# Half sums joined by GpSimd in the short convolution of a two-layer encoder trunk

## Chip, cores and metric

One core of a Trainium2 chip (trn2). The metric is the device time of one launch in microseconds (us). All data are float32; the matmuls run on float32r operands.

## What is computed

The reference is a trunk of two layers on 256 tokens of width 2048. Each half of a layer is a modulated RMS norm, a mixer or MLP, and a gated residual sum. The change touches layer 0's mixer only:

```python
def short_conv_mixer(h, w_in, w_conv, w_out):
    b_gate, c_gate, v = jnp.split(h @ w_in, 3, axis=-1)
    u = dwconv_centred(c_gate * v, w_conv)
    return (b_gate * u) @ w_out

# in the trunk, for every layer and both of its halves
shift, scale, gate = modulation(i, s)        # silu(c) @ ada_w[i, s] + ada_b[i, s]
h = rms_norm(x, norm_g[i, s]) * (1.0 + scale) + shift
x = x + gate * out
```

## The kernel before

Activations lie feature by token: 16 blocks of 128 features by 256 tokens. The work is a list of units. One unit is one output block of 128 features: 2048 inputs, so 16 weight blocks of 128x128, in two halves of eight blocks. One half of a unit's weights (128x1024, 512 KB) is one DMA into one of four slots of `raw`.

Precision is kept by splitting. For each half h, ScalarE writes `wh` = raw rounded to float32r (`hi`, line 740), and VectorE writes `wl` = raw - wh (`lo`, line 1495). Activations are split likewise into two planes of `hcat` or `hid`, an upper and a lower one. A product is then upper x wh + lower x wh + upper x wl. TensorE has two forms for it:

- `single` (`block`, lines 1241 to 1243): three matmuls of 256 columns for each weight block, all into the same 256 columns of PSUM. The product is complete there, and the consumer reads it straight out of PSUM.
- `unit` (lines 1175 and 1178): one matmul of 512 columns (wh against both planes side by side) and one of 256 (wl against the upper plane). PSUM then holds two half sums, in columns 0 to 255 and 256 to 511, which must be added behind it.

The convolution has 48 units, three for each feature block: c, v and b. The first 15 are the head, done together. The other 33 (11 feature blocks, function `conv`, first feature block peeled, then a loop) use `single`, as do 14 of the 16 units of the output projection (`conv_out`); its first two run as a pair in two banks of their own. Units alternate between two PSUM banks, `psm[0]` and `psm[1]`. Slots: `hi(h)` waits until TensorE is done with half h-4, `lo(h)` waits for `hi(h)`, TensorE for `lo(h)`, and the DMA into the slot for `lo(h-4)`. The order on every engine is written by hand: every engine walks the same list of stages, each with its own function for it, and semaphores tie them.

During these stages VectorE has a second job: one tile of the modulation matrix for each unit (`tile`, line 1508, 128x2048, 1024 KB by DMA into two slots), whose one-column result GpSimd saves (`keep`, line 579). For a feature block VectorE also computes pad = c*v (line 1639), two shifted taps into acc (lines 1560 and 1563), and acc*b (line 1648). ScalarE copies c out of PSUM (line 859), makes the middle tap (line 791) and the rounded result (line 796); GpSimd makes the lower plane of the result (`lower`, line 590). In `conv_out` VectorE adds gate*product to x (line 1668), ScalarE squares x (line 778), GpSimd sums the squares (`add_square`, line 585), and `keep` follows.

## Time and profile before

| what | value |
|---|---|
| median of 3 runs | 2591.91 us (2591.65 to 2592.6) |
| profiled execution, own time | 2591.94 us |
| profiled execution, span | 2590.2 us |
| TensorE busy | 2533.1 us, 98% of the span |
| VectorE busy | 2090.9 us, 81% |
| ScalarE busy | 1377.7 us, 53% |
| GpSimd busy | 623.5 us, 24% |
| mean rate from HBM | 262 GB/s |
| chain that ended last | PE 87%, DVE 7%, DMA 2%, ACT 2% |

PE is TensorE, PEld its weight load, DVE VectorE, ACT ScalarE, POOL GpSimd, SP the DMA queue's engine. A row's duration is from its start to its end; the distance between starts of neighbouring rows of one engine is a little less, since they overlap at their ends. The own time is 1.74 us above the span, and 0.03 us above the median.

### The profile page before, as it was taken

Reading aid. Unit: us, or ns where it says so; the run is one execution under the profiler, and the core shown is the slowest. Engines: PE = TensorE matmul, PEld = TensorE weight load, DVE = VectorE, ACT = ScalarE, POOL = GpSimd, SP = SyncE. Lnnn points to the kernel's source line nnn. Section 1 sums busy time; section 2 is a strip of 40 time slices with the busy share of each in tenths; the row PEclk is TensorE's granted clock in tenths of the full one; section 3 lists DMA queues with packets and bytes.
Section 4 is the critical chain, followed back from the end, with each engine's and each line's share of the span. In section 5 each row is a group of like instructions: output and inputs, shape, how many; then the busy total and the mean of one; then the engine's idle time right before and its main releaser. Section 6 shows DMA issues by size and latency. Waiting matters only on the chain.

```text
span 2590.2 us, 45227 instructions
## 1 busy us (share of the span) xinstructions
PE 2533.1 (98%) x15518; PEld 2247.1 (87%) x15518; DVE 2090.9 (81%) x2637; ACT 1377.7 (53%) x2149; POOL 623.5 (24%) x576
## 2 busy tenths in 40 slices
PE   7899999999999999999999999999999999999998
PEld 6789999888888888888888888888888888888887
DVE  7988998998989989758899899998899655555554
ACT  4444444544544445556677746776754444444454
POOL 0011132333343343320011141113333111121123
PEclk8999999999999999999999999999999999999999
DMA  9979997798888888746656697664588655555554
GB/s 395 417 294 365 364 379 297 274 359 313 333 332 325 328 330 327 269 152 210 207 197 202 195 360 282 203 199 151 171 292 318 202 187 187 188 185 191 189 185 139
DMA packets 163917, 679.71 MB, mean 262 GB/s; under 512 B 18720, under 2 KB 18976, under 8 KB 139072
## 3 DMA queue, kind: packets, MB, share of 16 engines
q1 hardware_dynamic: 163728, 677.75, 73.0%
q8 instruction: 83, 1.36, 0.2%
q14 instruction: 58, 0.48, 0.1%
q0 software_dynamic: 48, 0.13, 0.0%
HBM read 675.58 MB, written 2.23 MB: 262 GB/s over the span
## 4 chain that ended last, share of the span: by engine, by line
PE 87%; DVE 7%; DMA 2%; ACT 2%; issue 1%; DVEq 0%; SPq 0%; POOL 0%; ACTq 0%; POOLq 0%
PE psm L1175 47%; PE psm L1178 23%; PE psm L1241 4%; PE psm L1243 3%; PE psm L1242 3%; DVE wl L1495 2%; DMA xs<-in_ada 1%; PE psr L1215 1%; PE psm L1460 1%; DVE adat L1508 1%; ACT wh L740 1%; DVE xs L1508 1%; PE psr L1377 1%; DMA raw<-in_w 1%; PE psr L1460 0%
## 5 line engine op out<-in xcount | busy, mean ns | idle before, releaser
L1495 DVE TENSOR_TENSOR wl<-raw,wh 128x1024 fp32r<-128x1024 f32 x854 | 1073.0, 1258 | 256.1 <-ACT wh L740 250.3
L740 ACT ACTIVATE wh<-raw 128x1024 fp32r<-128x1024 f32 x854 | 900.5, 1056 | 406.5 <-PE psm L1178 181.5
L1175 PE MATMUL psm<-hcat,wh 128*128 128x512 f32 x3120 | 986.2, 397 | 0.0
L1178 PEld LDWEIGHTS psm<-hcat,wl 128*128 128x128 f32 x3120 | 586.1, 188 | 138.5
L1175 PE MATMUL psm<-hid,wh 128*128 128x512 f32 x2240 | 703.6, 395 | 0.2 <-DVE wl L1495 0.2
L1178 PE MATMUL psm<-hcat,wl 128*128 128x256 f32 x3120 | 613.3, 278 | 0.0
L1178 PEld LDWEIGHTS psm<-hid,wl 128*128 128x128 f32 x2240 | 420.8, 188 | 99.5
L1175 PEld LDWEIGHTS psm<-hcat,wh 128*128 128x128 f32 x3120 | 476.1, 189 | 6.1 <-issue 5.3
L1508 DVE CUSTOM_DVE_ANT_0 adat<-adat,cond 128x2048 f32<-128x2048 f32 x176 | 463.0, 2631 | 16.4 <-DMA adat<-in_ada 16.3
L1178 PE MATMUL psm<-hid,wl 128*128 128x256 f32 x2240 | 440.0, 278 | 0.0
L1175 PEld LDWEIGHTS psm<-hid,wh 128*128 128x128 f32 x2240 | 340.9, 189 | 0.4 <-DVE wl L1495 0.4
L631 POOL TENSOR_TENSOR x<-x,tt 128x256 f32 (+1 forms) x140 | 183.0, 1307 | 343.3 <-DVE tt L1692 343.3
L579 POOL COPY modc<-modt 128x1 f32 (+1 forms) x160 | 153.0, 956 | 416.5 <-DVE modt L1508 416.5
L641 POOL TENSOR_TENSOR hid<-tt,hid 128x256 f32 (+1 forms) x128 | 129.2, 1010 | 427.4 <-ACT hid L932 369.3
L745 ACT ACTIVATE ta<-psm 128x256 f32<-128x256 f32 x195 | 74.4, 382 | 247.4 <-PE psm L1178 247.4
L1241 PE MATMUL psm<-hcat,wh 128*128 128x256 f32 x592 | 170.8, 288 | 34.2 <-DVE hcat L1580 29.6
L1242 PE MATMUL psm<-hcat,wh 128*128 128x256 f32 x592 | 168.8, 285 | 0.0
L1243 PE MATMUL psm<-hcat,wl 128*128 128x256 f32 x592 | 168.7, 285 | 0.0
L745 ACT ACTIVATE ta<-psm,mods 128x256 f32<-128x256 f32 x140 | 66.4, 474 | 192.2 <-PE psm L1178 192.0
L1241 PEld LDWEIGHTS psm<-hcat,wh 128*128 128x128 f32 x592 | 114.7, 194 | 38.4 <-DVE hcat L1580 19.7
L1692 DVE SCALAR_TENSOR_TENSOR tt<-psm,mods,ta 128x256 f32<-128x256 f32 x140 | 67.0, 478 | 83.2 <-ACT ta L745 83.2
L1243 PEld LDWEIGHTS psm<-hcat,wl 128*128 128x128 f32 x592 | 114.9, 194 | 0.0
(257 smaller groups left out, 2575.3 us busy)
## 6 DMA issues: line engine op xcount, KB each, us to landing
raw<-in_w SPq DMA_DIRECT2D x866, 512.0 KB, 4.4
adat<-in_ada SPq DMA_DIRECT2D x176, 1024.0 KB, 6.8
dec<-running_sums SPq DMA_DIRECT2D x48, 256.0 KB, 6.3
xs<-in_ada SPq DMA_DIRECT2D x8, 1024.0 KB, 11.5
zs<-in_ada SPq DMA_DIRECT2D x8, 1024.0 KB, 11.7
normt<-running_sums SPq DMA_DIRECT2D x16, 256.0 KB, 4.7
x<-in_xT SPq DMA_DIRECT2D x4, 512.0 KB, 9.4
out<-x SPq DMA_DIRECT2D x4, 512.0 KB, 3.5
```

The source lines that it names most:

```text
L579: pool.tensor_copy(modc[:, bass.ds(a.v, 1)], modt[:, a % 2:a % 2 + 1]).then_inc(mod_copied, 1)
L631: pool.tensor_tensor(x[:, nn.v, :], x[:, nn.v, :], tt[:, v % 2, :], ALU.add).then_inc(stored, 1)
L641: pool.tensor_tensor(hid[:, jj.v, T:2 * T], tt[:, v % 2, :], hid[:, jj.v, 0:T].bitcast(F32), ALU.subtract).then_inc(stored, 1)
L740: act.activation(wh[:, h % 4, :], raw[:, h % 4, :], ACT.Copy).then_inc(hi_done, 1)
L745: act.activation(ta[:, v % 2, :], (bank or psm[v % 2])[:, 0:T], ACT.Copy, scale=scale).then_inc(copied, 1)
L1175: pe.matmul(both, wh[:, h % 4, (k + i) * P:(k + i + 1) * P], src[:, kb + i, :, :], start=(kb + i == 0), stop=(kb + i == KB - 1), skip_grou ...
L1178: mm = pe.matmul(bank[:, T:2 * T], wl[:, h % 4, (k + i) * P:(k + i + 1) * P], src[:, kb + i, 0, :], start=False, stop=(kb + i == KB - 1), ...
L1241: pe.matmul(out, hi_w, up, start=start, stop=False, skip_group_check=True)
L1242: pe.matmul(out, hi_w, down, start=False, stop=False, skip_group_check=True)
L1243: return pe.matmul(out, lo_w, up, start=False, stop=stop, skip_group_check=True)
L1495: dve.tensor_tensor(wl[:, h % 4, :], raw[:, h % 4, :], wh[:, h % 4, :].bitcast(F32), ALU.subtract).then_inc(lo_done, 1)
L1508: dve.tensor_tensor_reduce(t, t, cond[:, :], 1.0, 0.0, ALU.mult, ALU.add, column).then_inc(ada_done, 1)
```

## The change

The 33 units of `conv` and units 2 to 13 of `conv_out` (`halves_joined`) use `unit` in place of `single`. ScalarE copies both half sums of each of these units (128x512) out of PSUM into one of three SBUF buffers (`conv_halves`), GpSimd adds the two halves in place (`join`) and counts `joined`; VectorE's products then read the joined sums from SBUF, where they read PSUM before. PSUM banks are released by `copied` in place of `summed`. On VectorE the products move behind one more `lo`, and on ScalarE `hi(v*2+9)` moves ahead of the wait for the gated product. The diff, cut (a line beginning with @@ names the function):

```diff
+def halves_joined(k):
+
+    return 2 <= k < KB - 2
...
+        conv_halves = (normt[:, 0:2 * T], normt[:, 2 * T:4 * T], ta[:, :, :].rearrange("p c t -> p (c t)"))
...
+        joined = sem("joined")
...
                 keep(At(ADA_FIRST))
+                pool.sem_inc(joined, HEAD_UNITS)
+
+            def join(v, part):
+
+                at_least(pool, copied, v + 1)
+                both = conv_halves[part]
+                pool.tensor_tensor(both[:, 0:T], both[:, 0:T], both[:, T:2 * T], ALU.add).then_inc(joined, 1)
 
             def conv(u, j, n, ada_at, a):
                 tiles = adas(3 * n, ada_at, a)
                 for i in range(n):
-                    for t in tiles[3 * i:3 * i + 2]:
-                        keep(t)
+                    v, own = u + 3 * i, tiles[3 * i:3 * i + 3]
+                    join(v, 0)
+                    keep(own[0])
+                    join(v + 1, 1)
+                    keep(own[1])
+                    join(v + 2, 2)
                     lower(j + i)
-                    keep(tiles[3 * i + 2])
+                    keep(own[2])
 
             def conv_out(u, n, ada_at, a):
                 tiles = adas(4, ada_at, a)
                 for s in range(4):
+                    if halves_joined(n + s):
+                        join(At(u + s), (n + s) % 2)
+                    else:
+                        pool.sem_inc(joined, 1)
...
+            def copy_halves(v, part, read):
+
+                at_least(act, mm_done, v * 2 + 2)
+                at_least(act, summed, read)
+                act.activation(conv_halves[part], psm[v % 2][:, :], ACT.Copy).then_inc(copied, 1)
...
@@ def conv (scalar)
-                    at_least(act, mm_done, v * 2 + 2)
-                    at_least(act, summed, v - 4)
-                    act.activation(tt[:, jj % 2, :], psm[v % 2][:, 0:T], ACT.Copy).then_inc(copied, 3)
+                    copy_halves(v, 0, v - 1)
                     hi(v * 2 + 5)
                     if peeled:
                         head_upper(HEAD - 1)
                     hi(v * 2 + 6)
+                    copy_halves(v + 1, 1, v - 1)
                     hi(v * 2 + 7)
                     at_least(act, summed, v + 2)
                     middle(jj)
                     hi(v * 2 + 8)
+                    copy_halves(v + 2, 2, v)
+                    hi(v * 2 + 9)
                     at_least(act, summed, v + 3)
                     upper(jj)
-                    hi(v * 2 + 9)
@@ def conv_out (scalar)
                         hi(At(v * 2 + 4))
+                        if halves_joined(k):
+                            copy_halves(At(v), k % 2, At(v - 1))
...
                         hi(At(v * 2 + 5))
@@ def unit (tensor)
-                        at_least(pe, summed, u - lag)
+                        at_least(pe, released, u - lag)
@@ def conv (tensor)
+                peeled = not j.terms and j.c == HEAD
                 for s in range(3 * n):
-                    single(u + s, hcat)
+                    unit(u + s, hcat, released=summed if peeled and s < 2 else copied)
 
             def conv_out(u, n, ada_at, a):
                 for s in range(4):
-                    if n + s > 1:
-                        single(At(u + s), hid4, n + s if n + s < 4 else 1)
+                    if halves_joined(n + s):
+                        unit(At(u + s), hid4, lag=n + s if n + s < 4 else 1, released=copied)
+                    elif n + s > 1:
+                        single(At(u + s), hid4)
@@ def conv (vector)
-                    at_least(dve, copied, v + 3)
-                    dve.sem_inc(summed, 1)
                     lo(v * 2 + 5)
                     if peeled:
                         head_gated(HEAD - 1)
+                    at_least(dve, joined, v + 1)
+                    dve.sem_inc(summed, 1)
                     tile(own[0])
 
                     lo(v * 2 + 6)
-                    at_least(dve, mm_done, v * 2 + 4)
-                    dve.tensor_tensor(pad[:, k, 1:T + 1], tt[:, k, :], psm[(v + 1) % 2][:, 0:T], ALU.mult)\
+                    lo(v * 2 + 7)
+                    at_least(dve, joined, v + 2)
+                    dve.tensor_tensor(pad[:, k, 1:T + 1], conv_halves[0][:, 0:T], conv_halves[1][:, 0:T], ALU.mult)\
                         .then_inc(summed, 1)
-                    lo(v * 2 + 7)
                     tile(own[1])
 
                     taps(jj)
                     lo(v * 2 + 8)
+                    lo(v * 2 + 9)
                     at_least(dve, sc_conv, jj + 1)
-                    at_least(dve, mm_done, v * 2 + 6)
-                    dve.tensor_tensor(acc[:, k, :], acc[:, k, :], psm[(v + 2) % 2][:, 0:T], ALU.mult)\
-                        .then_inc(summed, 1)
-                    lo(v * 2 + 9)
+                    at_least(dve, joined, v + 3)
+                    dve.tensor_tensor(acc[:, k, :], acc[:, k, :], conv_halves[2][:, 0:T], ALU.mult).then_inc(summed, 1)
                     tile(own[2])
@@ def conv_out (vector)
+                    if halves_joined(k):
+                        lo(At(v * 2 + 5))
+                        at_least(dve, joined, At(v + 1))
+                        product = conv_halves[k % 2]
...
-                    if k:
+                    if k and not halves_joined(k):
                         lo(At(v * 2 + 5))
```

How this moves VectorE, in the peeled feature block (`hi`/`lo`, `tile` and the products; line numbers of the changed kernel are 36 to 40 higher). Before:

```order
L1508 ISA adat,modt<-adat,cond 128x2048
L1508 ISA modt 128x1
L1495 TENSOR_TENSOR wl<-raw,wh 128x1024
L1639 TENSOR_TENSOR pad<-tt,psm 128x256
L1495 TENSOR_TENSOR wl<-raw,wh 128x1024
L1508 ISA adat,modt<-adat,cond 128x2048
L1508 ISA modt 128x1
L1560 SCALAR_TENSOR_TENSOR acc<-pad,scw_c,acc 128x256
L1563 SCALAR_TENSOR_TENSOR acc<-pad,scw_c,acc 128x256
L1495 TENSOR_TENSOR wl<-raw,wh 128x1024
L1648 TENSOR_TENSOR acc<-acc,psm 128x256
L1495 TENSOR_TENSOR wl<-raw,wh 128x1024
```

Now:

```order
L1544 ISA adat,modt<-adat,cond 128x2048
L1544 ISA modt 128x1
L1531 TENSOR_TENSOR wl<-raw,wh 128x1024 x2
L1676 TENSOR_TENSOR pad<-normt 128x256
L1544 ISA adat,modt<-adat,cond 128x2048
L1544 ISA modt 128x1
L1596 SCALAR_TENSOR_TENSOR acc<-pad,scw_c,acc 128x256
L1599 SCALAR_TENSOR_TENSOR acc<-pad,scw_c,acc 128x256
L1531 TENSOR_TENSOR wl<-raw,wh 128x1024 x2
L1685 TENSOR_TENSOR acc<-acc,ta 128x256
L1544 ISA adat,modt<-adat,cond 128x2048
L1544 ISA modt 128x1
```

The two weight remainders (`wl`) now stand together, ahead of each product, and the products have no PSUM operand.

On GpSimd, from the head's `lower` to the end of the peeled feature block, with what each waits for. Before:

```order
L590 TENSOR_TENSOR hid<-acc,hid 128x256 [waits sc_hi] x4
L579 COPY modc<-modt 128x1 [waits ada_done] x3
L590 TENSOR_TENSOR hid<-acc,hid 128x256 [waits sc_hi]
L579 COPY modc<-modt 128x1 [waits ada_done]
L197 UNCONDITIONAL_BRANCH
```

Now (L597 is `lower`, L586 `keep`, L614 `join`):

```order
L597 TENSOR_TENSOR hid<-acc,hid 128x256 [waits sc_hi] x4
L586 COPY modc<-modt 128x1 [waits ada_done]
L614 TENSOR_TENSOR normt<-normt 128x256 [waits copied]
L586 COPY modc<-modt 128x1 [waits ada_done]
L614 TENSOR_TENSOR normt<-normt 128x256 [waits copied]
L586 COPY modc<-modt 128x1 [waits ada_done]
L614 TENSOR_TENSOR ta<-ta 128x256 [waits copied]
L597 TENSOR_TENSOR hid<-acc,hid 128x256 [waits sc_hi]
L586 COPY modc<-modt 128x1 [waits ada_done]
```

Three additions are new for each feature block, each behind a `keep` in GpSimd's order, the first of them also behind the head's last `lower`. In `conv_out` the join of a unit stands behind the `keep` of the unit before.

## Rows read from the trace of the kernel before

**Rows 1.** Windows behind the head, conv stage, projection; us, busy by engine, clock, DMA, GB/s

```profile
154.00:171.00 17.00, 13.71 (x101) 13.33 (x100) 14.54 (x18) 5.96 (x9) 4.56 (x5) 0.90 0.55 190
205.00:222.00 17.00, 17.00 (x144) 17.00 (x143) 15.07 (x17) 7.22 (x9) 3.05 (x4) 1.00 0.97 377
375.00:392.00 17.00, 17.00 (x144) 17.00 (x143) 17.00 (x16) 8.84 (x13) 7.66 (x7) 1.00 1.01 402
```

**Rows 2.** Lines of the conv stage, 205 to 339 us: busy, mean ns, idle before

```profile
L1495 DVE TENSOR_TENSOR wl<-raw,wh 128x1024 fp32r<-128x1024 f32 x48 | 57.9, 1221 | 12.3 <-ACT wh L740 12.3
...
L740 ACT ACTIVATE wh<-raw 128x1024 fp32r<-128x1024 f32 x47 | 49.1, 1055 | 34.5 <-DMA raw<-in_w 32.6 <-PE psm L1243 1.7
```

**Rows 3.** Timeline of PE, conv stage: two starts of the three-matmul block, one block apart

```profile
239.92 0.28 PE L1241 MATMUL psm<-hcat,wh 128*128 128x256 f32 x1
...
240.28 0.28 PE L1241 MATMUL psm<-hcat,wh 128*128 128x256 f32 x1
```

**Rows 4.** Timeline of PE in an MLP stage: two-matmul blocks, ten blocks apart

```profile
700.19 0.63 PE L1175 MATMUL psm<-hcat,wh 128*128 128x512 f32 x2
...
703.67 0.63 PE L1175 MATMUL psm<-hid,wh 128*128 128x512 f32 x2
```

**Rows 5.** Timeline of DVE, one conv channel block: start us, duration us, operation

```profile
239.62 0.42 DVE L1648 TENSOR_TENSOR acc<-acc,psm 128x256 f32<-128x256 f32 x1
241.56 1.23 DVE L1495 TENSOR_TENSOR wl<-raw,wh 128x1024 fp32r<-128x1024 f32 x1 [1.53 <-ACT wh L740]
242.71 2.29 DVE L1508 CUSTOM_DVE_ANT_0 adat<-adat,cond 128x2048 f32<-128x2048 f32 x1
...
244.92 2.35 DVE L1495 TENSOR_TENSOR wl<-raw,wh 128x1024 fp32r<-128x1024 f32 x2
...
254.78 0.48 DVE L1560 SCALAR_TENSOR_TENSOR acc<-pad,scw_c,acc 128x256 f32<-128x256 f32 x1
...
255.81 1.22 DVE L1495 TENSOR_TENSOR wl<-raw,wh 128x1024 fp32r<-128x1024 f32 x1
256.95 0.41 DVE L1648 TENSOR_TENSOR acc<-acc,psm 128x256 f32<-128x256 f32 x1
```

**Rows 6.** Timeline of POOL in the same stretch

```profile
240.79 0.74 POOL L590 TENSOR_TENSOR hid<-acc,hid 128x256 f32 x1 [2.81 <-ACT hid L796]
245.16 1.02 POOL L579 COPY modc<-modt 128x1 f32 x1 [3.63 <-DVE modt L1508]
...
255.01 0.29 POOL L579 COPY modc<-modt 128x1 f32 x1 [4.35 <-DVE modt L1508]
```

**Rows 7.** Timeline of DVE in the output projection

```profile
376.02 0.47 DVE L1668 SCALAR_TENSOR_TENSOR x<-psm,mods,x 128x256 f32<-128x256 f32 x1
376.41 1.21 DVE L1495 TENSOR_TENSOR wl<-raw,wh 128x1024 fp32r<-128x1024 f32 x1
377.55 2.82 DVE L1508 CUSTOM_DVE_ANT_0 adat<-adat,cond 128x2048 f32<-128x2048 f32 x1
...
381.44 0.47 DVE L1668 SCALAR_TENSOR_TENSOR x<-psm,mods,x 128x256 f32<-128x256 f32 x1
```

**Rows 8.** Timeline of POOL in the output projection

```profile
377.02 1.20 POOL L585 TENSOR_TENSOR ss<-ss,normt 128x256 f32<-128x256 f32 x1 [0.88 <-ACT normt L778]
```

**Rows 9.** Timeline of DVE behind the head

```profile
161.39 2.28 DVE L1508 CUSTOM_DVE_ANT_0 adat<-adat,cond 128x2048 f32<-128x2048 f32 x1
...
163.60 1.75 DVE L1495 TENSOR_TENSOR wl<-raw,wh 128x1024 fp32r<-128x1024 f32 x1
```

**Rows 10.** Timeline of POOL behind the head

```profile
162.07 2.20 POOL L590 TENSOR_TENSOR hid<-acc,hid 128x256 fp32r<-128x256 f32 x1 [3.57 <-ACT hid L796]
```

**Rows 11.** Timeline of ACT behind the head

```profile
157.53 0.37 ACT L859 ACTIVATE tt<-psm 128x256 f32<-128x256 f32 x1
```

**Rows 12.** Timeline of PE: the conv stage's fourth unit starts

```profile
165.74 0.39 PE L1241 MATMUL psm<-hcat,wh 128*128 128x256 f32 x1 [0.21 <-DVE pad L1639]
```

**Rows 13.** Timeline of PE: first matmul of the output projection

```profile
339.28 0.28 PE L1241 MATMUL psr<-hid,wh 128*128 128x256 f32 x1
```

More of the change, by code:

```diff
@@ L876, in conv_out @@
                         hi(At(v * 2 + 4))
+                        if halves_joined(k):
+                            copy_halves(At(v), k % 2, At(v - 1))
+                        else:
+                            act.sem_inc(copied, 1)
                         hi(At(v * 2 + 5))
+                    else:
+                        act.sem_inc(copied, 1)
                     if k == 0:
@@ L886, in conv_out @@
                     scaled_block(1, k)
-                act.sem_inc(copied, 4)
             def squared(nn, layer):
@@ L1160, in _, with unit @@
         def _(pe):
-            def unit(u, src, ready=None, fresh=False, bank=None, lag=1):
+            def unit(u, src, ready=None, fresh=False, bank=None, lag=1, released=summed):
                 bank = bank or psm[u % 2]
@@ L1665, in conv_out @@
                         modulation(1, 0)
-                    at_least(dve, mm_done, At(2 * U_SCOUT + 4 if k < 2 else v * 2 + 2))
-                    bank = conv_out_bank[k] if k < 2 else psm[v % 2]
-                    dve.scalar_tensor_tensor(out=x[:, k, :], in0=bank[:, 0:T], scalar=mods[:, 0, 2, k:k + 1],
+                    if halves_joined(k):
+                        lo(At(v * 2 + 5))
+                        at_least(dve, joined, At(v + 1))
+                        product = conv_halves[k % 2]
+                    else:
+                        at_least(dve, mm_done, At(2 * U_SCOUT + 4 if k < 2 else v * 2 + 2))
+                        product = conv_out_bank[k] if k < 2 else psm[v % 2]
+                    dve.scalar_tensor_tensor(out=x[:, k, :], in0=product[:, 0:T], scalar=mods[:, 0, 2, k:k + 1],
                                              in1=x[:, k, :], op0=ALU.mult, op1=ALU.add).then_inc(summed, 1)
-                    if k:
+                    if k and not halves_joined(k):
                         lo(At(v * 2 + 5))
```

## The prediction

> **What bounds the kernel now.** I read the windows of the two stages first. In the lower two TensorE is busy for all 17 us of 17 at full clock, VectorE for 15.07 in the convolution and for all 17.00 in the output projection, and the DMA engines for 0.97 and more of the time at 377 and 402 GB/s [rows 1]. So three resources stand close together, and making one faster is worth only what the next one leaves. The grouped lines show who waits: ScalarE's `hi` for its DMA (32.6 us in 134), VectorE's `lo` for `hi` (12.3 us) [rows 2]; TensorE for nobody. The timelines then give the rates.
>
> TensorE starts a three-matmul block every 0.36 us [rows 3], so a `single` unit takes 16 x 0.36 = 5.76 us and a feature block of three units 17.28. In the two-matmul form ten blocks take 3.48 us [rows 4], 0.348 each: 5.57 a unit, 16.71 for three.
>
> VectorE [rows 5], from start to start: a `lo` 1.14 (376.41 to 377.55 [rows 7]), a `tile` 2.21, a product 0.33 (0.41 long, less 0.08 of overlap as at 376.02 [rows 7]), the two taps with their wait 1.03 (254.78 to 255.81). A feature block is 6 x 1.14 + 3 x 2.21 + 2 x 0.33 + 1.03 = 15.16 us. The rest of its 17.3 us is idle: 1.53 us of it before the `lo` at 241.56, because `hi(v*2+9)` stands behind ScalarE's wait for the gated product.
>
> GpSimd matters through VectorE. Its two-input addition takes 0.74 us when VectorE is idle [rows 6]. Issued at 377.02, inside a `lo` that runs to 377.55, it takes 1.20 and ends at 378.22, and the `tile` that starts at 377.55 takes 2.82 instead of 2.29 [rows 5, 7, 8]. It waited for the operation under way, then ran alone, and VectorE lost 0.53 us. A `keep` is itself nearly free to VectorE, but it also waits for the end of an operation: 0.29 us at 255.01, but 1.02 at 245.16, where a `lo` ran until about 246.1 [rows 5, 6].
>
> **The sum.** *TensorE.* 33 + 12 = 45 units each need 5.76 - 5.57 = 0.19 us less: 8.6 us is the most that the change can gain. A rule of the Trainium skill speaks against even that: "TensorE: Matmul & The Clock Gate", section "Back-to-back issue gap", gives a matmul its columns over 2.4 GHz plus 2.5 ns, so three times 256 columns against 512 + 256 would differ by 2.5 ns a block, and the gain would be an estimated 1.8 us in all. The rows show 12 ns a block, and I go by the rows.
>
> *ScalarE.* In `conv` 33 copies of 128x512 take the place of 11 of 128x256 (0.37 us each [rows 11]); per column a 128x1024 `hi` costs 1.055 us, so a 512-column copy lies between 0.37 and 1.06; I take 0.6. That is at most 3 us more in an iteration in which ScalarE is busy under half [rows 1]; nothing on the path. Moving `hi(v*2+9)` ahead of the wait takes away VectorE's 1.53 us of idling: VectorE can now run 15.16 us of work back to back.
>
> *GpSimd and VectorE, convolution.* Three joins for each feature block. VectorE is idle for almost nothing any more, so each lands in one of its operations and costs 0.53 or more, and so now does `lower`, which ran in the idle stretch before [rows 6]. Two of the joins cost more: GpSimd has a `keep` ahead of them, the `keep` waits for the first `lo` behind the `tile`, and by the time it is done the second `lo` has started; the join runs behind that one, from its end for 0.67 us (377.55 to 378.22), and VectorE stands at its wait for `joined`. With some 0.06 us for the semaphore that is 0.73. The new products have no PSUM operand; from the nearest rows (0.33, 0.39) they cost the same within 0.06. So an iteration takes 15.16 + 2 x 0.53 + 2 x 0.73 = 17.68 us, above the 16.71 TensorE needs and above the 17.28 of now. Bounds for four GpSimd additions: below nothing is lost (every one in a gap) and TensorE's 16.71 rules; above, each join misses one more `lo` of 1.14 somewhere, 18.8.
>
> The Trainium skill ("SBUF — State Buffer", section "SBUF: two separate sides") says that a GpSimd operation and a VectorE operation with two SBUF inputs hold the shared port by turns, each for its whole instruction. The rows agree in kind but give 0.53 where a whole addition would be 0.74; with the page's reading the whole change would come to an estimated +16 us, the third rival's size.
>
> *Behind the head.* GpSimd's `lower` for the last head block ran from 162.07 to 164.27, blocked by the `tile` at 161.39 [rows 9, 10]. Now VectorE must wait for the first join before that `tile`, and GpSimd has `lower`, a `keep` and then the join in this order: 162.07 + 0.74 + 0.29 [rows 6] + 0.74 = 163.9 with the steps between. Then `tile` (2.21) and `lo` (1.14) end at 167.4, where that `lo` ended at 163.60 + 1.75 = 165.35. TensorE's fourth unit needs it, and started at 165.74 [rows 12]: +1.7 us.
>
> *To the output projection.* From the fourth unit to the first matmul of `conv_out` it took 339.28 - 165.74 = 173.54 us [rows 12, 13]; ten iterations at 17.68 are 176.8: +3.3. In every iteration TensorE then waits 17.68 - 16.71 = 0.97 us for the fifth `lo`; the last such wait falls into the projection's first pair: +1.0.
>
> *Output projection.* VectorE's period there is 5.42 us [rows 7]: two `lo`, a product of 0.39, a `tile` and 0.53 for `add_square`. It is below TensorE's 5.76, so it had a little room. Now a join comes on top, again behind a `keep` and again awaited: 5.42 + 0.73 = 6.15, less up to 0.06 for the PSUM operand, 6.1, above TensorE's 5.57. Twelve units have it. Behind the end of the pair VectorE has two products (0.8), two `lo` (2.3), two tiles (4.4), two additions' delays (1.1), and some 2.3 that, laid out the same way, it is late by from the last feature block: the first `lo` of unit 4 is done 10.9 us on, that of unit 15 11 x 6.1 = 67.1 later, and unit 15 takes 5.76: 83.8 against 14 x 5.76 = 80.6. +3.1.
>
> Sum: 1.7 + 3.3 + 1.0 + 3.1 = 9.1 us. The profiled execution took 2591.94 us, the median is 2591.91, so the same: **2601.0 us**. Everything later is only shifted; units 14 and 15 stay `single` and have no tile, so VectorE catches up before the norm.
>
> **Rivals.** About 0.2% (5 us) is what a measurement of this kernel can tell from no change.
>
> *A, the joins cost 0.53 and no wait.* If GpSimd catches the gap between two `lo`, an iteration is 15.16 + 4 x 0.53 = 17.28, as now, and the projection's period 5.9. Then 1.7 behind the head, -0.7 from small stalls of now that go, 0.6 in the pair and 0.9 in the projection: about 2594.4. For it: the addition needs only VectorE's next boundary. Against: the `keep` ahead of it uses that boundary up [rows 6]. Chance 0.25.
>
> *B, the other side: TensorE stays the bound.* If the additions fall into gaps, or a product from SBUF is much cheaper, VectorE's iteration stays below 16.71. That decides: at most 1.55 us for the four additions, under 0.39 each. The gain is then 8.6 - 1.7 = 6.9: 2585.0, faster. For it: 1.53 us of idling goes, and DMA has kept up with a unit every 5.42 us at 402 GB/s [rows 1, 7], where 5.57 needs 2.1 MB/5.57 = 377. Against: the 0.53 at 377.55, and VectorE busy for 15.07 of 17 us even now [rows 1], so gaps are rare. Chance 0.15.
>
> *C, the waits chain.* VectorE's wait for `joined` also holds the `lo`s queued behind it, and a stall of TensorE behind the head can lower its clock again: the window behind the head has a mean granted clock of 0.90, all others 1.00 [rows 1], so part of it ran at 1.2 GHz instead of 2.4 after an idle stretch. If each addition costs a full 0.74 an iteration takes 18.1 us: +7.5 over the ten, 1.7, 1.4 and, at 6.3 a unit, +5.4 in the projection: 2608. Chance 0.1.
>
> That the change doesn't do what it says is excluded by the order of the instructions; it can only be hidden.
>
> **How the numbers follow.** The forecast 0.5 (its own range 2597.5 to 2605), A 0.25, B 0.15, C 0.1. Slower by over 5 us is the forecast, nearly whole, and C: 0.58. Within: A and the low edge of the forecast, 0.27. Faster: B, 0.15. The range leaves out the lower part of B and the upper of C: 2588 to 2606.
>
> **What would show it.** Right: between 205 and 330 us TensorE in the 0.348 rhythm with one idle stretch of about 1 us for each feature block, waiting for `wl`; VectorE over 95% busy or waiting for the join; an iteration of 17.7; joins of 1.2 us and longer; the fourth unit at 167.4; 6.1 us for a unit of the projection, its first matmul near 345. Wrong: TensorE 17.00 of 17 there and an iteration of 16.7 (B), or 17.3 (A); joins of 0.74 with no row of VectorE longer than before; or waits of `hi` for `raw` that reach TensorE, a bound by DMA that I hold for excluded.

## The result: 15.6 us slower, and the profile after

The changed kernel takes 2607.87 us, the median of six runs (2604.47 to 2609.39), against 2592.26 of the kernel before in as many (the three of the section before, 2591.91, are among them): a ratio of 1.0061, 95% interval 1.0051 to 1.0071, so 15.6 us slower. The forecast was 2601.0, +9.1, with a range up to 2606. The profiled execution took 2607.64 us, close to the median; its span is 15.7 us longer than before.

The head of the page of the changed kernel:

```profile
span 2605.9 us, 43950 instructions
...
PE 2533.1 (97%) x14798; PEld 2211.8 (85%) x14798; DVE 2102.9 (81%) x2637; ACT 1392.3 (53%) x2183; POOL 711.3 (27%) x621
```

720 matmuls are gone, and TensorE's busy time is what it was, 2533.1: part of the rest now runs at half the clock (below). Whether that makes up the whole difference was not worked out. GpSimd has 88 us more. The three windows of [rows 1], now, with the same columns (span of the window, busy us of TensorE, its weight load, VectorE, ScalarE and GpSimd, then granted clock, DMA share and GB/s), and three short ones behind waits of TensorE:

```profile
154.00:171.00 17.00, 9.80 (x51) 8.27 (x50) 9.71 (x13) 6.10 (x9) 5.68 (x7) 0.92 0.33 111
205.00:222.00 17.00, 16.45 (x95) 14.16 (x94) 15.24 (x16) 8.29 (x11) 7.66 (x7) 1.00 0.99 359
375.00:392.00 17.00, 16.60 (x94) 14.16 (x93) 15.11 (x14) 8.18 (x14) 13.85 (x10) 1.00 0.94 362
...
169.30:172.00 2.70, 2.70 (x8) 2.32 (x9) 2.08 (x3) 0.62 (x2) 1.58 (x1) 0.50 0.87 346
...
229.00:233.00 4.00, 3.30 (x18) 2.92 (x19) 4.00 (x4) 1.82 (x4) 1.13 (x1) 1.00 0.99 268
...
434.00:438.00 4.00, 3.92 (x20) 3.95 (x21) 4.00 (x4) 3.15 (x5) 3.54 (x3) 0.58 0.92 317
```

TensorE, which was busy for all 17.00 us in the convolution and the projection, now is for 16.45 and 16.60; in the window of the projection VectorE fell from 17.00 to 15.11 and GpSimd rose from 7.66 to 13.85. The DMA moves less (362 GB/s for 402) and isn't the bound: with the additions left out it moved 385 there (experiment 1). The timeline of TensorE shows the waits:

```profile
169.29 1.22 PE L1208 MATMUL psm<-hcat,wh 128*128 128x512 f32 x2 [3.61 <-DVE wl L1531]
...
229.70 0.72 PE L1208 MATMUL psm<-hcat,wh 128*128 128x512 f32 x2 [0.89 <-DVE wl L1531]
...
434.08 0.36 PE L1274 MATMUL psm<-hid,wh 128*128 128x256 f32 x1 [2.61 <-DVE x L1708]
434.27 0.28 PE L1275 MATMUL psm<-hid,wh 128*128 128x256 f32 x1
434.39 0.28 PE L1276 MATMUL psm<-hid,wl 128*128 128x256 f32 x1
...
435.88 0.41 PE L1275 MATMUL psm<-hid,wh 128*128 128x256 f32 x1
436.10 0.41 PE L1276 MATMUL psm<-hid,wl 128*128 128x256 f32 x1
```

Three things are to be seen. The fourth unit (169.29) waits 3.61 us for a `lo`. Once in each feature block between 205 and 340 us there is a wait of 0.56 to 0.89 us (here 0.89), again for a `lo`. And at 434.08 stands one that the forecast did not have: 2.61 us for VectorE's product of the projection, and soon behind it matmuls 0.21 to 0.22 us apart where 0.12 us is the full rate: the first five start 0.12 to 0.19 us apart, and the slow stretch goes from 434.63 to 438.02. The short windows show the granted clock: 0.50 behind the wait at 169.29 and 0.58 behind the one at 434.08, so nearly all of it at the lower of the two levels, 1.2 GHz; 1.00 behind a wait of a feature block.

Why VectorE is late shows in its timeline, one feature block and one product of the projection:

```profile
224.72 2.28 DVE L1544 CUSTOM_DVE_ANT_0 adat<-adat,cond 128x2048 f32<-128x2048 f32 x1
...
227.57 0.87 DVE L1599 SCALAR_TENSOR_TENSOR acc<-pad,scw_c,acc 128x256 f32<-128x256 f32 x1 [0.15 <-DVE acc L1596]
228.36 2.35 DVE L1531 TENSOR_TENSOR wl<-raw,wh 128x1024 fp32r<-128x1024 f32 x2
...
233.17 2.89 DVE L1531 TENSOR_TENSOR wl<-raw,wh 128x1024 fp32r<-128x1024 f32 x2
236.93 2.29 DVE L1544 CUSTOM_DVE_ANT_0 adat<-adat,cond 128x2048 f32<-128x2048 f32 x1 [0.87 <-POOL normt L614]
...
242.13 0.43 DVE L1676 TENSOR_TENSOR pad<-normt 128x256 f32<-128x256 f32 x1 [0.62 <-POOL normt L614]
242.47 2.28 DVE L1544 CUSTOM_DVE_ANT_0 adat<-adat,cond 128x2048 f32<-128x2048 f32 x1
...
433.44 0.48 DVE L1708 SCALAR_TENSOR_TENSOR x<-normt,mods,x 128x256 f32<-128x256 f32 x1 [0.61 <-POOL normt L614]
```

and GpSimd in the same stretch (L597 is `lower`, L586 `keep`, L614 the join):

```profile
227.42 0.73 POOL L614 TENSOR_TENSOR ta<-ta 128x256 f32<-128x256 f32 x1
231.87 1.97 POOL L597 TENSOR_TENSOR hid<-acc,hid 128x256 f32 x1 [3.72 <-ACT hid L824]
233.79 1.18 POOL L586 COPY modc<-modt 128x1 f32 x1
234.93 1.73 POOL L614 TENSOR_TENSOR normt<-normt 128x256 f32<-128x256 f32 x1
239.38 1.03 POOL L586 COPY modc<-modt 128x1 f32 x1 [2.73 <-DVE modt L1544]
240.37 1.73 POOL L614 TENSOR_TENSOR normt<-normt 128x256 f32<-128x256 f32 x1
```

Read the two side by side. `lower` at 231.87 waits for the end of VectorE's `tile` (one operation of 2.2 us that starts at 230.96) and holds the pair of `lo` behind it, which takes 2.89 us instead of 2.35: 0.54. The `keep` at 233.79 then waits for the end of the first of these `lo`; the second has started when the join is issued at 234.93, and the join is done 1.73 us later, so VectorE stands for 0.87. The next join does the same and is awaited for 0.62 us; the third falls into a tap (0.87 instead of 0.48: 0.39). The 15.16 us of VectorE's own work, these four, and twice the 0.08 of overlap that a wait loses come to 15.16 + 0.54 + 0.87 + 0.62 + 0.39 + 0.16 = 17.74; from 224.72 to 242.47 it took 17.75. The mechanism of the forecast is there as written. In the grouped lines of 200 to 345 us:

```profile
L1544 DVE CUSTOM_DVE_ANT_0 adat<-adat,cond 128x2048 f32<-128x2048 f32 x25 | 57.1, 2285 | 8.2 <-POOL normt L614 8.2
...
L1676 DVE TENSOR_TENSOR pad<-normt 128x256 f32<-128x256 f32 x8 | 3.4, 426 | 5.0 <-POOL normt L614 5.0
```

VectorE, which waited 12.3 us for `hi` before [rows 2], waits 13.2 us for joins.

**Where the 15.7 us came in**, from the starts of four matmuls in the two timelines (of before: 143.27, [rows 12], [rows 13] and 431.44; of after: 144.88, 169.29, 347.74 and 447.15), against the forecast:

| stretch | before | after | more | forecast |
|---|---|---|---|---|
| start to the convolution's first unit | 143.27 | 144.88 | 1.6 | 0 |
| to its fourth unit | 22.47 | 24.41 | 1.9 | 1.7 |
| to the projection's first matmul | 173.54 | 178.45 | 4.9 | 3.3 |
| to the norm's first matmul | 92.16 | 99.41 | 7.3 | 4.1 |
| to the end | 2158.8 | 2158.8 | 0.0 | 0 |

The 1.6 us of the first row are not the change's. The same wait of TensorE, 1.88 us for `hcat`, ends at 130.74 us before and at 130.86 now; the windows behind it, before and then now:

```profile
130.70:134.00 3.30, 3.27 (x27) 3.27 (x28) 3.30 (x2) 0.75 (x1) 0.00 (x0) 1.00 1.05 418
130.70:134.00 3.30, 3.14 (x14) 3.14 (x15) 3.30 (x3) 0.00 (x0) 0.00 (x0) 0.52 1.04 416
```

The granted clock is 1.00 in one execution and 0.52 in the other, and 14 matmuls start there for 27.

### The profile page after: what moved, and what is told of

Its sections match the earlier page's. It is cut to its first block, busy times and chain, and to the rows that moved or that the text cites. A ratio compares the mean times of both kernels' runs of the same rounds, so it can differ in the third digit from the quotient of the medians.

```text
span 2605.9 us, 43950 instructions
## 1 busy us (share of the span) xinstructions
PE 2533.1 (97%) x14798; PEld 2211.8 (85%) x14798; DVE 2102.9 (81%) x2637; ACT 1392.3 (53%) x2183; POOL 711.3 (27%) x621
## 4 chain that ended last, share of the span: by engine, by line
PE 77%; DVE 8%; POOL 4%; issue 4%; DMA 3%; ACT 2%; DVEq 0%; POOLq 0%; ACTq 0%; SPq 0%
PE psm L1208 47%; PE psm L1211 23%; DVE wl L1531 3%; POOL normt L614 2%; PE psr L1248 2%; DMA xs<-in_ada 1%; DVE adat L1544 1%; DMA adat<-in_ada 1%; POOL ss L592 1%; PE psm L1496 1%; POOL modc L586 1%; DVE xs L1544 1%; POOL hid L597 1%; ACT wh L762 1%; PE psr L1413 1%
## 5 line engine op out<-in xcount | busy, mean ns | idle before, releaser
L1208 PE MATMUL psm<-hcat,wh 128*128 128x512 f32 x3648 | 1155.0, 398 | 14.7 <-DVE wl L1531 9.9
L1208 PE MATMUL psm<-hid,wh 128*128 128x512 f32 x2432 | 764.7, 396 | 2.4 <-DVE wl L1531 2.3
L1211 PE MATMUL psm<-hcat,wl 128*128 128x256 f32 x3648 | 718.0, 278 | 0.0
L1208 PEld LDWEIGHTS psm<-hcat,wh 128*128 128x128 f32 x3648 | 557.6, 189 | 22.9 <-issue 22.3
L1211 PEld LDWEIGHTS psm<-hid,wl 128*128 128x128 f32 x2432 | 456.9, 188 | 108.0
L1211 PE MATMUL psm<-hid,wl 128*128 128x256 f32 x2432 | 477.8, 278 | 0.0
L1208 PEld LDWEIGHTS psm<-hid,wh 128*128 128x128 f32 x2432 | 370.2, 189 | 4.2 <-DVE wl L1531 4.2
L586 POOL COPY modc<-modt 128x1 f32 (+1 forms) x160 | 155.1, 969 | 331.8 <-DVE modt L1544 331.8
L1567 DVE TENSOR_TENSOR tt<-ta,psm 128x256 f32<-128x256 f32 x120 | 49.8, 415 | 62.6 <-ACT ta L767 62.6
L592 POOL TENSOR_TENSOR ss<-ss,normt 128x256 f32<-128x256 f32 x60 | 76.4, 1274 | 56.8 <-ACT normt L806 54.7
L965 ACT ACTIVATE hid<-tt 128x256 f32 (+1 forms) x120 | 50.2, 419 | 59.6 <-DVE tt L1762 56.5
L597 POOL TENSOR_TENSOR hid<-acc,hid 128x256 f32 (+1 forms) x16 | 26.0, 1623 | 199.0 <-ACT hid L824 199.0
```

Source lines behind the costliest of these rows:

```text
L586: pool.tensor_copy(modc[:, bass.ds(a.v, 1)], modt[:, a % 2:a % 2 + 1]).then_inc(mod_copied, 1)
L592: pool.tensor_tensor(ss[:, :], ss[:, :], sq[:, m % 2, :], ALU.add).then_inc(ss_added, 1)
L1208: pe.matmul(both, wh[:, h % 4, (k + i) * P:(k + i + 1) * P], src[:, kb + i, :, :], start=(kb + i == 0), stop=(kb + i == KB - 1), skip_grou ...
L1211: mm = pe.matmul(bank[:, T:2 * T], wl[:, h % 4, (k + i) * P:(k + i + 1) * P], src[:, kb + i, 0, :], start=False, stop=(kb + i == KB - 1), ...
```

## The experiments

Beside each stands the median of its runs and the ratio to the kernel before, timed on the same chip (its median was 2591.27 to 2592.05 in the three batches). Differences between kernels of different batches are good to about 1 us; against its own kernel before, the changed one has +15.6 us. A diff is against the changed kernel unless it says otherwise.

**1. No addition.** GpSimd only counts, so every product of these 45 units is made from half of its sum.

```diff
@@ join (gpsimd)
-                pool.tensor_tensor(both[:, 0:T], both[:, 0:T], both[:, T:2 * T], ALU.add).then_inc(joined, 1)
+                pool.sem_inc(joined, 1)
```

> The additions on GpSimd are left out (the semaphore is counted in their place), so every product of these 45 units is made from half of its sum. Theory, GpSimd's additions make VectorE the bound: a feature block falls from 17.80 us to TensorE's 16.7, a projection unit from 6.14 to 5.57, unit 14's wait for its bank and the 1.9 us behind the head go; about 2587 us, some 21 below the changed kernel. Rival, the longer chain (copy, semaphore, one more lo ahead of the product) or the DMA of the weights is the bound: within 4 us of the changed kernel's 2607.9.

Measured: 2585.58 us, ratio 0.998 (0.9971 to 0.999). The windows of the convolution and the projection:

```profile
205.00:222.00 17.00, 17.00 (x100) 14.87 (x99) 16.85 (x17) 9.71 (x13) 4.96 (x5) 1.00 1.02 416
375.00:392.00 17.00, 17.00 (x99) 14.82 (x98) 17.00 (x17) 10.09 (x16) 10.87 (x7) 1.00 0.99 385
```

TensorE is never idle, a feature block takes 16.72 us, the projection 89.9 us from its first matmul to the norm's (92.2 before), and the DMA gives 416 GB/s in the convolution. So in these two stages ScalarE's copies of 128x512 and the new order cost nothing that reaches the end. The medians lie 22.3 us apart (21.3 by each kernel's distance from its own kernel before), and that is what the additions cost; in the two traces 1.5 us of the distance is the start again, which is not theirs.

**2 and 3. The addition's size.** One column, then 128 of the 256; the rest of each sum stays half.

```diff
@@ join (gpsimd)
-                pool.tensor_tensor(both[:, 0:T], both[:, 0:T], both[:, T:2 * T], ALU.add).then_inc(joined, 1)
+                pool.tensor_tensor(both[:, 0:1], both[:, 0:1], both[:, T:T + 1], ALU.add).then_inc(joined, 1)
```
```diff
+                pool.tensor_tensor(both[:, 0:T // 2], both[:, 0:T // 2], both[:, T:T + T // 2], ALU.add).then_inc(joined, 1)
```

> The additions stay with all their waits and their place in GpSimd's order, but add one column of 256 (the rest of each sum is left half). Theory, it is the time in which the addition holds VectorE up: a feature block near 16.7 us, product's wait for joined from 0.63 to 0.2 or less; 2587 to 2592 us. Rival, the place in the order (behind a keep, behind a second lo, awaited) costs by itself: a feature block stays above 17.3 and the time above 2600.

> GpSimd adds 128 of the 256 columns (half of each sum's correction is left out). Theory, the cost follows the addition's own time, so it lies between one column (2586.5) and 256 (2607.9): an addition of about 0.42 us instead of 0.74, a feature block of 17.0 us, about 2597. Rival, a fixed cost for a queued addition: nearer to 2607.9 than 3 us, or as one column.

Measured: 2586.54 us with one column (ratio 0.9983, 0.9973 to 0.9992), 2596.59 with 128 (1.0021, 1.0011 to 1.0031), 2607.87 with all 256. GpSimd's joins in the grouped lines, with one column:

```profile
L614 POOL TENSOR_TENSOR normt<-normt 128x1 f32<-128x1 f32 x17 | 17.2, 1009 | 0.0
L614 POOL TENSOR_TENSOR ta<-ta 128x1 f32<-128x1 f32 x9 | 2.7, 305 | 1.5 <-ACT ta L773 1.5
```

and with 128:

```profile
L614 POOL TENSOR_TENSOR normt<-normt 128x128 f32<-128x128 f32 x16 | 23.2, 1453 | 0.0
...
L614 POOL TENSOR_TENSOR ta<-ta 128x128 f32<-128x128 f32 x8 | 3.7, 459 | 0.0
```

A join of one column into `normt`, behind a `keep`, takes 1.01 us in the mean, nearly all of it waiting, and the kernel is as fast as without it. So neither the wait for a boundary nor the semaphore is what costs: the columns do, since VectorE stands still while they are added. From the fourth unit to the projection it takes 167.6, 170.4 and 178.5 us with 1, 128 and 256 columns, and 167.5 without any. The cost isn't in proportion to the columns, because only what VectorE needs beyond TensorE's 16.71 us is seen: with 128 columns a block of VectorE takes 16.92.

**4. The release of two banks.** Units 14 and 15 of the projection are `single` and wait for `summed`, VectorE's product of two units before. Here they wait for `copied`, which ScalarE gives.

```diff
-            def single(u, src, lag=1):
+            def single(u, src, lag=1, released=summed):
...
-                        at_least(pe, summed, u - lag)
+                        at_least(pe, released, u - lag)
...
-                        single(At(u + s), hid4)
+                        single(At(u + s), hid4, released=copied)
```

> Units 14 and 15 of the projection wait for their PSUM bank on the copy (copied) instead of on the product (summed). Theory, the 2.6 us of idling ahead of unit 14 and the 1.6 us at half clock behind it come from this wait alone: 4 us less, 2603.5 to 2604.5. Rival, the weights' remainders of unit 14 come as late: no change within 1 us.

Measured: 2603.22 us in four runs, ratio 1.0044 (1.0027 to 1.0061), 4.7 less than the changed kernel, or 3.7 by each one's distance from its own kernel before. Its interval overlaps the changed kernel's, so the trace has to carry this one. The waits of TensorE from 345 to 448 us, in the changed kernel:

```profile
PE psm L1274 <- DVE x L1708: 2.6, 1, 2.6
PE psm L1208 <- DVE wl L1531: 2.0, 7, 0.3
PE psr L1274 <- DVE wl L1531: 0.6, 1, 0.6
```

and here (us in total, times, the longest):

```profile
PE psm L1274 <- DVE wl L1531: 0.3, 1, 0.3
```

The one wait of 2.6 us became one of 0.3, its matmuls stay 0.12 us apart at a granted clock of 1.00, and from the first matmul of the projection to the norm's it takes 96.06 us instead of 99.41: 3.35 less. What is left, 96.06 - 92.16 = 3.9, stands against the forecast's 4.1 for the pair and the projection.

**5. The `keep` behind the join.** On GpSimd each `keep` of both stages, and the last one of the head, moves behind the next join. The `keep` ahead of a join then saves an older tile and is done while GpSimd would wait for ScalarE's copy anyway (`own[0] - 1` is the tile of the unit before).

```diff
@@ conv (gpsimd)
                     join(v, 0)
-                    keep(own[0])
+                    keep(own[0] - 1)
                     join(v + 1, 1)
-                    keep(own[1])
+                    keep(own[0])
                     join(v + 2, 2)
+                    keep(own[1])
                     lower(j + i)
-                    keep(own[2])
@@ conv_out (gpsimd)
                         pool.sem_inc(joined, 1)
+                    if s == 0 or tiles[s - 1] is not None:
+                        keep(a + (s - 1))
...
-                    keep(tiles[s])
```

> On GpSimd each keep moves behind the next join, nothing else. Theory, an awaited addition costs 0.2 us more than one that only takes a turn, and needs VectorE's next boundary: a feature block from 17.80 to 17.3 us and a projection unit from 6.14 to 5.9; 2599 to 2602 us. Rival, whole additions serialise with VectorE wherever they stand: within 2 us of 2607.9.

Measured: 2597.21 us (2594.41 to 2604.87), ratio 1.0023 (1.0013 to 1.0032): 10.7 less than the changed kernel (9.7 by the distances from the kernels before), and 1.8 below the range foreseen. VectorE here (the profiled execution is one of the two longest, for a stop at 800 us that is told below; only rows ahead of it are used):

```profile
241.40 0.73 DVE L1599 SCALAR_TENSOR_TENSOR acc<-pad,scw_c,acc 128x256 f32<-128x256 f32 x1
...
246.88 3.43 DVE L1531 TENSOR_TENSOR wl<-raw,wh 128x1024 fp32r<-128x1024 f32 x2
...
252.44 2.89 DVE L1531 TENSOR_TENSOR wl<-raw,wh 128x1024 fp32r<-128x1024 f32 x2
255.25 0.41 DVE L1676 TENSOR_TENSOR pad<-normt 128x256 f32<-128x256 f32 x1
```

and GpSimd:

```profile
245.50 2.04 POOL L597 TENSOR_TENSOR hid<-acc,hid 128x256 f32 x1 [3.33 <-ACT hid L824]
247.51 1.72 POOL L613 TENSOR_TENSOR normt<-normt 128x256 f32<-128x256 f32 x1
...
250.68 2.43 POOL L613 TENSOR_TENSOR normt<-normt 128x256 f32<-128x256 f32 x1 [0.33 <-ACT normt L773]
```

No row of VectorE waits for a join any more. Two GpSimd additions (`lower` and a join) lie in the pair of `lo` at 246.88, 3.43 us instead of 2.35, and one in the pair at 252.44, 2.89: 0.54 each; the third join falls into a tap (241.40, 0.73 us where 0.49 was usual: 0.24). 15.16 + 3 x 0.54 + 0.24 = 17.0, and a block takes 17.0 us. So 0.54 is what an addition costs VectorE when it is not awaited and falls between two `lo`, and the wait behind a `keep` was worth 0.8 us a block. Unit 14's wait for its bank is still there, 2.25 us long.

**6. Both together.** The diffs of experiments 4 and 5 in one kernel:

```diff
-                        single(At(u + s), hid4)
+                        single(At(u + s), hid4, released=copied)
...
-                    keep(own[0])
+                    keep(own[0] - 1)
```

> The edits of e3_release and e4_keep_behind together. Theory, they act at different places (e3 behind unit 13, e4 in every unit) and add up: 2597.2 - 3 to 4 us, 2593 to 2594.5, still not below the kernel before. Rival, with shorter periods unit 14's wait is gone by itself: 2597.

Measured: 2594.17 us, ratio 1.001 (1.0 to 1.0019), as foreseen. The trace lists no wait of TensorE between 335 us and the norm. With both mended, what the additions hold is still enough to use up the 8.6 us that the matmuls give: from the convolution's first unit to its fourth it takes 24.7 us (22.5 before), to the projection 170.6 (173.5), to the norm 93.9 (92.2).

**7. Only the convolution.** The projection as before the change.

```diff
@@ halves_joined
-    return 2 <= k < KB - 2
+    return False
...
-                        single(At(u + s), hid4)
+                        single(At(u + s), hid4, n + s if n + s < 4 else 1)
```

> The change in the convolution's 33 units only; the projection's units are again single, read out of PSUM, with no joins. Theory: a feature block stays at 17.8 us, the projection goes back to what it took before plus 1 us of lateness, and unit 14's stall goes with the joins; 5 to 6 us less than the changed kernel, 2602 to 2603. Rival, the projection was harmless and only the convolution costs: within 2 us of 2607.9.

Measured: 2599.05 us, ratio 1.0028 (1.0017 to 1.0039), 3 less than foreseen. The projection takes 92.99 us here from its first matmul to the norm's, 0.8 more than before the change; a block takes 17.80 again. Of the distance to the changed kernel's trace, 9.2 us, 6.4 is the projection. Of the rest, 1.4 us lie ahead of the convolution, which begins at 143.44 us in this execution, with the clock at 1.00 behind the wait at 130.88, and at 144.88 in the changed kernel's. Another 1.4 lie behind the norm's first matmul (2157.4 us to the end for 2158.8), in stages that the two kernels share; their cause is open.

**8. VectorE adds.** GpSimd's `conv` has its order of before; ScalarE copies the first half only, and VectorE adds the second half straight out of PSUM. The projection is as in experiment 7.

```diff
@@ conv (gpsimd)
-                    join(v, 0)
...
-                act.activation(conv_halves[part], psm[v % 2][:, :], ACT.Copy).then_inc(copied, 1)
+                act.activation(conv_halves[part][:, 0:T], psm[v % 2][:, 0:T], ACT.Copy).then_inc(copied, 1)
...
-                    unit(u + s, hcat, released=summed if peeled and s < 2 else copied)
+                    unit(u + s, hcat, released=summed if peeled and s < 2 else joined)
...
+            def join(v, part):
+                at_least(dve, copied, v + 1)
+                half = conv_halves[part][:, 0:T]
+                dve.tensor_tensor(half, half, psm[v % 2][:, T:2 * T], ALU.add).then_inc(joined, 1)
```

> Convolution as in e5_conv_only, but GpSimd adds nothing: ScalarE copies only the first half sum, and VectorE adds the second to it straight out of PSUM, three additions of 0.33 us a feature block; the projection is as before the change. Theory, VectorE then has 15.16 + 3 x 0.33 + 0.53 = 16.7 us of work, as much as TensorE's 16.71, and nothing waits behind the head; the gain of the two-matmul form stands: 4 to 6 us faster than before the change, 2586 to 2588. Rival, three more operations on the busiest engine cost as much as GpSimd's: 2592 or more.

Measured: 2589.9 us, ratio 0.9991 (0.9981 to 1.0): blocks of 16.72 us as foreseen, and 2 to 4 us lost elsewhere. TensorE:

```profile
163.46 1.19 PE L1205 MATMUL psm<-hcat,wh 128*128 128x512 f32 x2 [7.59 <-POOLq L608]
```

and GpSimd:

```profile
158.98 0.73 POOL L597 TENSOR_TENSOR hid<-acc,hid 128x256 fp32r<-128x256 f32 x1 [4.77 <-ACT hid L821]
163.27 0.73 POOL L597 TENSOR_TENSOR hid<-acc,hid 128x256 fp32r<-128x256 f32 x1 [3.57 <-ACT hid L821]
```

TensorE's third unit now waits for `joined`, and the head's 15 counts of it (line 608) stand in GpSimd's list behind the head's `lower`s. A count that nobody waited for had become one that TensorE waits for, 7.59 us long.

**9. The counts first.** Experiment 8, with the head's counts at the start of GpSimd's list (diff against experiment 8).

```diff
+                pool.sem_inc(joined, HEAD_UNITS)
...
                 keep(At(ADA_FIRST))
-                pool.sem_inc(joined, HEAD_UNITS)
```

> e7_vector_adds, but the head's 15 counts of joined are given at the start of GpSimd's list and not behind its five lower operations, where TensorE's third convolution unit waited 7.6 us for them. Theory, that stall falls back to the 3.3 us it was before the change, and the rest of e7 stays: 4 us less than e7's 2589.9, 2585 to 2587. Rival, VectorE is at 99% from here on and the conv stage's pace comes from it alone, so that the start does not matter: 2589 to 2590.

Measured: 2586.28 us (2585.22 to 2587.46), ratio 0.9978 (0.9969 to 0.9987): 5.8 us faster than the kernel before, 21.6 faster than the changed one. The windows of [rows 1] in this kernel:

```profile
154.00:171.00 17.00, 13.16 (x60) 11.19 (x59) 14.80 (x20) 7.60 (x12) 4.55 (x5) 0.80 0.54 186
205.00:222.00 17.00, 17.00 (x100) 14.82 (x99) 16.85 (x21) 7.77 (x11) 4.46 (x4) 1.00 0.93 365
375.00:392.00 17.00, 17.00 (x144) 17.00 (x143) 17.00 (x16) 8.77 (x13) 6.96 (x6) 1.00 1.00 387
```

and VectorE's timeline:

```profile
208.88 1.76 DVE L1528 TENSOR_TENSOR wl<-raw,wh 128x1024 fp32r<-128x1024 f32 x1
210.57 0.41 DVE L1658 TENSOR_TENSOR normt<-normt,psm 128x256 f32<-128x256 f32 x1
210.90 1.21 DVE L1528 TENSOR_TENSOR wl<-raw,wh 128x1024 fp32r<-128x1024 f32 x1
```

An addition on VectorE itself, out of PSUM, takes 0.33 us from start to start (210.57 to 210.90) where one on GpSimd takes 0.54 of VectorE's time, and 0.70 to 1.06 when it is awaited (waits of 0.62 to 0.98, and the 0.08 of overlap). A block is 15.16 + 3 x 0.33 + 0.54 for `lower` = 16.69 us of VectorE, just TensorE's 16.71: both are full. Behind the head TensorE still waits 3.8 us once.

**10. The head's wait.** Experiment 9, with the first copy and addition ahead of the head's fourth product of five (diff against experiment 9).

```diff
@@ conv (scalar)
+                    copy_halves(v, 0, v - 1)
                     if peeled:
                         head_upper(HEAD - 2)
-                    copy_halves(v, 0, v - 1)
@@ conv (vector)
+                    join(v, 0)
                     if peeled:
                         head_gated(HEAD - 2)
-                    join(v, 0)
```

> e10, and in the peeled feature block the first copy and its addition stand ahead of the head's fourth gated product on ScalarE and VectorE. Theory, TensorE's third unit then waits for its weights' remainder alone, about 1 us instead of 3.3, with no stretch at half clock behind it: 1.5 to 3 us less than e10, 2583 to 2585. Rival, VectorE, which is full, hands the time back in the following units: no change from e10.

Measured: 2586.65 us, ratio 0.9977 (0.9968 to 0.9986): nothing gained on experiment 9, where 1.5 to 3 us were expected. Window 154 to 171:

```profile
154.00:171.00 17.00, 11.95 (x59) 9.86 (x58) 13.34 (x18) 7.93 (x13) 4.68 (x6) 0.92 0.46 171
```

The clock is 0.92 instead of 0.80, but in place of one wait of 3.84 us TensorE has three, 1.63, 0.91 and 2.51, the first and the last for VectorE's additions: 5.05 together. From the convolution's first unit to the projection it takes 191.4 us, and took 190.8 in experiment 9. So nothing was gained even up to there; the edit moved VectorE's work about, and VectorE, at 16.69 us of work for TensorE's 16.71, had no room for it. That last step is argued.

## Why the prediction was right in kind, and where it failed

**What bounds it: right.** The rhythm behind the gain of at most 8.6 us is real (experiment 1 shows it, with TensorE at 17.00 of 17, and is 5.7 us faster than the kernel before although it takes 0.7 us longer behind the head), and VectorE is held up by GpSimd by more than that. The likeliest case came, slower; its size was short by 6.5 us, and the range missed by 1.9.

**Rhythm of two matmuls: right.** The rows' 12 ns a block held: blocks of three units took 16.72 us in experiment 1, where 17.28 was the rhythm of before. By the 2.5 ns of the Trainium skill ("TensorE: Matmul & The Clock Gate", "Back-to-back issue gap") they would have taken an estimated 17.16; that section gives the figure for an isolated matmul, and the stream of this kernel does not follow it.

**The convolution: right in kind, 1.6 us short.** An iteration was put at 17.68 and took 17.80 (142.44 us for the eight between TensorE's waits at 211.83 and 354.27): in the block above the awaited joins cost 0.95 and 0.70 us instead of 0.73 each, the third 0.39 instead of 0.53. That is 1.2 us over ten; the other 0.4 comes in once, and where was not traced. It isn't the half clock behind the fourth unit: in experiment 7 that unit ran at a granted clock of 1.00, and the stretch took the same 178.5 us, since VectorE sets the pace there. What each addition costs was the term sized too small: four of them came to 2.58 us with the overlap, for 2.52.

**Behind the head: right.** +1.9 for +1.7. The `tile` behind the first join starts at 165.72 us, which without the late start is 164.1, for the 163.9 worked out.

**Projection: one step failed.** The steps for the pair and the twelve units held: 6.1 us a unit, +4.1 forecast, +3.9 in experiment 4; the pair's share, put at 1.0, was 0.8 in experiment 7. What failed is the sentence behind the sum, that units 14 and 15 "stay `single` and have no tile, so VectorE catches up before the norm". They are `single`, and so their bank is released by VectorE's product and not by ScalarE's copy; and by then VectorE is behind, so unit 14 waits 2.61 us and then runs most of its first half at the half clock. The sum had this wait at nothing; experiment 4 puts it at 3.35 us in its trace, 3.7 to 4.7 by the medians. Without it the time would have been inside the range. I had counted how late VectorE's `lo` would be and had not asked of each other thing that TensorE waits for, how late that would be. The diff shows it: of two forms, one had its release changed.

**The start: 1.6 us, not forecast, and not the change's.** The convolution's first unit starts at 144.88 us in place of 143.27, before anything of the change has run there. Twelve kernels have a trace. In six of them, the kernel before among them, the granted clock from 130.7 to 134 us is 1.00 and that unit starts between 143.27 and 143.86; in the other six it is 0.51 to 0.70 and the unit starts between 144.45 and 144.88. No edit sorts them so. How the six executions behind each median divide isn't on record, so how much of the 15.6 us between the medians this is stays open; an estimate from these starts is 1.6 at most.

**Two long executions.** Experiment 3 had four executions, and experiment 5 two, that lie 4 to 8 us above their medians (experiments 1 and 2 had one each), and the profiled ones of 3 and 5 are among them. Both show one stop of TensorE, 4.96 us and 5.17, at the same point of an unchanged stage, 366.5 us behind the norm's first matmul, for which the profile names no releaser, and the half clock behind it. What stops it is open. It has nothing to do with the change, but if the other long executions have it too, it lifts the median of experiment 3.

**The rivals.** A (0.53, no wait, 2594.4) is what experiment 6 built: 2594.17. That was the change without its two bad neighbours in the order. The total agrees closer than the parts do: A's block was 17.28 us and measured 17.0, since one of the four additions cost 0.24 instead of 0.53, while the stretch behind the head took 2.2 us more than before instead of 1.7. B needed less than 0.39 for each addition: 0.54 was measured, and where the additions were left out (experiment 1) or went to VectorE for 0.33 (experiment 9), B's 2585 came, at 2585.58 and 2586.28. C came nearest to the measured time (2608), and mostly not for its reason: it had 0.74 for each addition, and a block of 18.1 us where 17.80 was measured. Its other half, a lower clock behind the head's stall, did come (0.50 behind the fourth unit) and cost nothing, as experiment 7 shows. The reading of the Trainium skill ("SBUF — State Buffer", "SBUF: two separate sides") that an operation holds the port for the whole instruction would also have come to an estimated +16, and the trace speaks against the size that it gives: 0.54 us of delay for an instruction of 0.73, in every pair of `lo` that met one. The total of +16 agreed by chance: the wait behind a `keep`, unit 14's bank and the slow start made up the rest.

## What to carry to other kernels

When an addition moves to GpSimd next to a VectorE that is nearly 90% busy, price it by what VectorE loses while it holds (0.54 us for 128x256 here), and look at what stands ahead of it in GpSimd's order: behind a running VectorE operation, a one-column copy uses up the boundary and turns a hold into a wait. If VectorE must read the result anyway, let it add out of PSUM: 0.33 us. And when one form of a step gets a new release, list every neighbour that still waits for the old one; a wait costs nothing only as long as the engine behind it is early.

## What the runs showed of the hardware that I had not expected

A one-column GpSimd operation waits as long as a big one: an addition of 128x1 into `normt` took 1.01 us in the mean behind a `keep` and a `keep` 0.83, though where VectorE was between operations they took 0.19 and 0.28. Two GpSimd operations issued back to back behind a running VectorE operation do not use one boundary: each takes one of its own, as at 231.87, 233.79 and 234.93. The 0.15 us in which VectorE stands between its two taps do let both through: the `keep` at 227.17 took 0.28 us and the join at 227.42 came right behind it, 0.73 long.

And the length of a wait alone did not tell TensorE's clock. The same wait of 1.88 us was followed by a granted clock of 1.00 in the kernel before and of 0.52 in the changed one (windows from 130.7 to 134). A wait of 3.6 us at the convolution's third unit was followed by 1.00 in the changed kernel (159.8 to 163) and by 0.50 in experiment 7 (158.4 to 163). The 2.61 us at 434.08 were followed by full rate for 0.5 us and the half clock for 3.4; the 0.56 to 0.89 us of the feature blocks in the changed kernel never were (granted clock 1.00 in the window from 229 to 233). So two profiled executions can lie 1.5 us apart for one such wait and nothing else, and a half clock costs only where TensorE sets the pace.
